# Expert weights through two queues: places 1, 3 and 5 of a round loaded by GpSimd, the other four by SP

## What is computed

```python
N_EXPERTS = 8; TOP_K = 2; EXPERT_FF = 3584

def _swiglu(x, w1, w3, w2):
    return (jax.nn.silu(x @ w1) * (x @ w3)) @ w2

def _moe(x, w_router, w1, w3, w2):
    logits = (xt @ w_router).astype(jnp.float32)
    top_v, top_e = lax.top_k(logits, TOP_K)
    gates = jax.nn.softmax(top_v, axis=-1)
    # every expert e: y[tokens that chose e] += gate * _swiglu(x[those tokens], w1[e], w3[e], w2[e])
```

## Time and profile before

| | us |
|---|---|
| median of the runs | 3134.4 |
| lowest and highest | 3132.83, 3137.07 |
| the profiled execution | 3133.49 |
| its span, first to last instruction | 3131.8 |
| from the first expert's first up product to the end of the last | 850.8 to 1677.0 |
| TensorE busy in the span | 3082.3 |
| DMA queue q1 (SP) | 703.62 MB |
| DMA queue q0 (GpSimd) | 8.02 MB |

### The profile page before, as it was taken

The page is one execution under the profiler, slowest core; times in us unless marked ns, Lnnn a source line. Parts: engine busy times, 40 slices in busy tenths (PEclk is TensorE's granted clock), DMA queues, the critical chain, the costliest instruction groups (busy, mean ns, idle before and its releaser), DMA issues.

```text
span 3131.8 us, 79620 instructions
## 1 busy us (share of the span) xinstructions
PE 3082.3 (98%) x36280; PEld 2622.5 (84%) x36280; DVE 1326.7 (42%) x2660; ACT 445.9 (14%) x1079; POOL 53.9 (2%) x87
## 2 busy tenths in 40 slices
PE   9999999999999999999998999999999999999998
PEld 6686894978599999999997967898995976999894
DVE  2252566543201110111014665754566565654465
ACT  1250000042111111111111001211100001111100
POOL 0000000000000000000000000000000000000000
PEclk9999999999999999999999999999999999999999
DMA  7434443432699999999996444433444444434442
GB/s 261 143 114 161 162 161 145 186 132 106 251 416 423 426 426 427 426 426 426 427 426 243 176 164 177 151 144 136 175 175 152 179 160 162 176 135 162 151 172 87
DMA packets 63239, 716.24 MB, mean 229 GB/s; under 512 B 7584, under 2 KB 9248, under 8 KB 11904
## 3 DMA queue, kind: packets, MB, share of 16 engines
q1 hardware_dynamic: 59328, 703.62, 57.0%
q0 software_dynamic: 1152, 8.02, 0.7%
q10 hardware_dynamic: 2624, 2.65, 0.4%
HBM read 711.38 MB, written 1.05 MB: 227 GB/s over the span
## 4 chain that ended last, share of the span: by engine, by line
PE 93%; DMA 4%; DVE 2%; ACT 1%; issue 1%; POOL 0%; SPq 0%; POOLq 0%; DVEq 0%; ACTq 0%
PE psum L647 50%; PE psum L838 13%; PE psum L768 10%; PE psum L848 7%; PE psum L904 4%; DMA weight_ring<-in_experts 4%; PE psum L1166 1%; PE psum L868 1%; PE psum L1259 1%; PE psum L813 1%; PE psum L685 1%; PE psum L681 1%; PE psum L975 0%; PE psum L680 0%; POOL statistics L566 0%
## 5 line engine op out<-in xcount | busy, mean ns | idle before, releaser
L647 PE MATMUL psum<-arena,weight_ring 128*128 128x128 f32 (+1 forms) x6752 | 938.6, 299 | 9.0 <-DVE arena L2302 5.3
L647 PEld LDWEIGHTS psum<-arena,weight_ring 128*128 128x128 f32 x6752 | 881.2, 192 | 53.4 <-issue 14.9
L838 PE MATMUL psum<-arena,weight_ring 128*64 128x80 f32 x14336 | 531.3, 233 | 8.8 <-ACT arena L1461 6.3
L838 PEld LDWEIGHTS psum<-arena,weight_ring 128*64 128x64 f32 x14336 | 510.0, 137 | 13.4 <-ACT arena L1461 7.6
L647 PE MATMUL psum<-weight_ring,arena 128*128 128x128 f32 (+4 forms) x3264 | 494.7, 309 | 2.7 <-DVE arena L2071 2.7
L647 PEld LDWEIGHTS psum<-weight_ring,arena 128*128 128x128 f32 x3264 | 431.4, 191 | 55.5 <-issue 34.3
L1877 DVE TENSOR_TENSOR arena<-arena,psum 128x80 f32<-128x80 f32 x224 | 53.4, 238 | 691.0 <-ACT arena L1451 691.0
L848 PE MATMUL psum<-arena,weight_ring 128*64 128x80 f32 x7168 | 281.7, 233 | 2.3 <-issue 2.3
L848 PEld LDWEIGHTS psum<-arena,weight_ring 128*64 128x64 f32 x7168 | 263.0, 137 | 2.7 <-issue 2.7
L1451 ACT ACTIVATE arena<-psum 128x80 f32<-128x80 f32 x224 | 53.4, 238 | 642.8 <-PE psum L838 642.8
L904 PE MATMUL psum<-weight_ring,arena 128*128 128x512 f32 x320 | 138.8, 592 | 0.0
(11 more groups left out here) (292 smaller groups left out, 2367.8 us busy)
## 6 DMA issues: line engine op xcount, KB each, us to landing
weight_ring<-in_experts SPq DMA_DIRECT2D x224, 1536.0 KB, 14.5
weight_ring<-in_ffn_up SPq DMA_DIRECT2D x44, 2048.0 KB, 7.7
weight_ring<-in_second_wide SPq DMA_DIRECT2D x42, 2048.0 KB, 7.8
weight_ring<-in_first_wide SPq DMA_DIRECT2D x35, 2048.0 KB, 8.8
weight_ring<-in_ffn_down SPq DMA_DIRECT2D x20, 2048.0 KB, 7.8
weight_ring<-in_dense_up SPq DMA_DIRECT2D x11, 2048.0 KB, 8.0
weight_ring<-in_dense_down SPq DMA_DIRECT2D x5, 2048.0 KB, 8.0
weight_ring<-in_ffn_down SPq DMA_DIRECT2D x4, 1024.0 KB, 5.2
```

The costliest lines, as they stand in the source:

```text
L647: m = pe.matmul(o, lhs, rhs, start=i == 0, stop=i == len(terms) - 1)
L838: mm = pe.matmul(psum[g * STRIP:(g + 1) * STRIP, q % 4, m * CAP:(m + 1) * CAP], w[:, m, k, g * STRIP:(g + 1) * STRIP], chosen[:, k, :], st ...
```

## The change

Places 0, 2, 4 and 6 of a round are still loaded by SP, through the same loops with a step of two. Places 1, 3 and 5 are loaded by GpSimd with the same waits, from loops of the same form, which stand in its program behind the load of `late_gate` and ahead of the first layer norm root after the experts. Buffers, semaphores, bytes and every other engine's program stay.

```diff
-            for q in range(ROUND):
+            for q in range(0, ROUND, 2):
                 sp.wait_ge(unit_used, MOE_START - SLOTS + 1 + q // 2)
                 sp.dma_start(expert_unit(q), a["experts"][q * P:(q + 1) * P, :]).then_inc(expert_loaded[q], 16)
             def load_round(e, g):
-                for q in range(ROUND):
+                for q in range(0, ROUND, 2):
                     sp.wait_ge(expert_used, ROUND * (ROUNDS * e + g) + q - ROUND + 1)
                     sp.dma_start(expert_unit(q), ...).then_inc(expert_loaded[q], 16)
...
+            def load_round(e, g):
+                for q in range(1, ROUND, 2):
+                    pool.wait_ge(expert_used, ROUND * (ROUNDS * e + g) + q - ROUND + 1)
+                    pool.dma_start(expert_unit(q), a["experts"][bass.ds((e * EXPERT_UNITS + ROUND * g + q) * P, P), :]).then_inc(expert_loaded[q], 16)
...
                     pool.dma_start(late_gate, ...)
+                if l == 1:
+                    for q in range(1, ROUND, 2):
+                        pool.wait_ge(unit_used, MOE_START - SLOTS + 1 + q // 2)
+                        pool.dma_start(expert_unit(q), a["experts"][q * P:(q + 1) * P, :]).then_inc(expert_loaded[q], 16)
+                    with pool.Fori(1, ROUNDS) as g:
+                        load_round(0, g)
+                    with pool.Fori(1, EXPERTS) as e:
+                        with pool.Fori(0, ROUNDS) as g:
+                            load_round(e, g)
                 for h in range(HALVES):
                     layernorm_root(l, 1, h)
```

## The result

| | before | after |
|---|---|---|
| median of the runs | 3134.1 us (4 runs, 3132.8 to 3137.1) | 3161.9 us (4 runs, 3160.2 to 3164.3) |
| profiled execution | 3133.5 us, span 3131.8 | 3162.6 us, span 3160.9 |

The ratio is 1.0085, with a 95% interval of 1.0071 to 1.0099: slower by 0.85%, far over the 0.2% that can be told from no change. The forecast was 3138 us with a range up to 3152; the time lies outside it.

The account below looks back on a forecast made before the run. Transfers were taken to bound the expert stage. Issuing, rate and start-up at 0 and order at +3.5 us gave 3133.5 + 3.5 = 3137.0 us, with 0.9 us for the median 3138 us; range 3131 to 3152 us.

Parts of the forecast that it names:

- What bounds the kernel: Expert stage: from the third or fourth expert on, transfers are the bound, by 1.2 us per expert over TensorE.
- Issuing at 0: Expert stage: GpSimd sits idle for 854.9 us, nothing useful queues behind the new waits, so issuing there costs 0.
- Rate at 0: Expert stage: both queues together move 427 GB/s as one does; 0 taken, ends -6.7 and +18 us, 8.0 us per cent.
- the engines get slower: Rival, expert stage: GpSimd's descriptors must be written and fetched, slowing the engines; 1% is 8.0 us, 3146 us; chance 0.10.
- Order at +3.5 us: Stage's end: GpSimd's units land early and SP's late, leaving TensorE more work after the last landing; +3.5 us.
- three SP loads left: Pattern at the stage's end: 219 lands at T - 7.38 us and five units remain, 9.2 us after T; +5.9 us.
- Start-up at 0: Expert's end: GpSimd's later start, some 4 us on busy engines, is just hidden by the cover; 0.
- a cover of 4.9 us: Expert's end: about 4.9 us of data the engines still hold when slots are freed again at 1579.7 us.
- that rival: Engines run dry after each expert, TensorE's delay shrinking the cover; about 10 us over seven ends plus 3.5, 3148 us; chance 0.27.
- the rate rival: Expert stage: the engines get slower with GpSimd's descriptors; 1% is 8.0 us; chance 0.10.
- 422 or less with visible dips after each expert: Sign in the stage's rate, in GB/s, that the engines run dry; lower everywhere would mean slower engines.
- The sign for the order: Rate stands and the last load leaves TensorE two or more units; its waits come at even places, SP's.

Follow-up runs that it names:

- the kernel with one load held back: Kernel before, all expert loads by SP, but the first load after an expert's start waits for two more used units: 3155.5 us, ratio 1.0068.
- even split: Against the kernel before, SP loads even units and ScalarE odd ones, counted over the whole run: 3136.5 us, ratio 1.0008.
- one place: Against the kernel before, GpSimd loads only place 3 of every round, 32 of 224 loads: 3137.8 us, ratio 1.0009.
- the disorder kept away from the ends: Against the kernel before, ScalarE loads places 1, 3 and 5 in rounds 1 and 2 of each expert only, SP the rest: 3135.0 us, ratio 1.0002.
- the swap: The change with places exchanged, GpSimd loading 0, 2, 4, 6 and SP 1, 3, 5: 3153.2 us, ratio 1.0061 against the kernel before.

## Why the prediction was wrong, point by point

**What bounds the kernel: right.** The transfers bound the stage, and each microsecond in which the engines are dry is paid: 2.5 us of gap, 2.7 us of a longer expert, in the kernel with one load held back.

**Issuing at 0: right for the stage, wrong for the program.** The conditions and the root behind them cost nothing. But I counted what a GpSimd load costs where it is issued and not what it leaves behind for the end. The drain, 1.49 us in the kernel before, had a cover of 3.5 us; 7.84 us more exposed 4.5. The step that failed is "Cost 0" under issuing; I had not looked at GpSimd's last instruction.

**Rate at 0: half right.** Two busy queues can run at 426 GB/s (even split, one place). But in this split packets were slow after each gap, 7.6 us in all by the packets' own times, near the 8.0 us that I gave to 1%. It is neither in the rate of two GpSimd loads beside SP's nor in a slower engine everywhere, and the rival "the engines get slower" had another mechanism in mind: the last 76 us of the expert ran at 427. Most of it falls where at most two expert loads were in flight, so it belongs to the engines' running dry more than to the rate. A slip besides: eight times 102.1 and 3 is 819.8 and not 819.5 us, so the most that could be gained was 6.4 us and not 6.7.

**Order at +3.5 us: right mechanism, too small and put in one place only.** At the stage's end the measured +4.5 us (9.2 left instead of 4.7) lies between my +3.3 and the +5.9 us for three SP loads left; the chain with five units after the wait is that pattern. That its 9.2 us came out to the tenth is luck: the five units took 17.9 us and not 16.6, because six sets of down products and not five lay in them, and began 8.8 us before the last landing and not 7.4. For the same reason the 3.3 us that I set against it were too few; my own gave 4.7. The failing step is that this term was booked once, at the end. The same delay of TensorE against the transfers comes at each expert's end, where it takes the cover. I wrote this down as a rival and left it out of the sum. The runs show it as the main thing: with the order kept, or the disorder kept away from the ends, nothing is lost.

The Trainium skill (DMA: Bandwidth & Descriptors, Queues, rings and completion order) says that each engine takes turns, packet by packet, between the queues that have work for it. By that rule the queue with three places of seven gets half the engines while both have loads, and the trace agrees: from 1231 to 1242 us q0 took 50.2% and q1 50.5% of the engines' time, and the loads take 12.3 us to landing against 16.3. The same page's Rules for kernel authors say that spreading transfers over issuing engines doesn't help bandwidth and saves issue time only. That there was nothing to gain the runs bear out; here the spreading cost 0.85%.

**Start-up at 0: the step that failed most.** It rested on a cover of 4.9 us, read in a kernel whose order the change itself alters. With it spent, both queues' starts are exposed. The rival's figures were a cover of 1.4 us for SP's first load and 1.8 us for GpSimd's; measured gaps are 1.35 and 0.91 us in the third expert, so both covers were shorter than thought: SP's own start is exposed too, which I had left out. From its issue to full engines GpSimd's load took 3.4 us (SP's 2.0), near the some 4 us of the earlier trace rows. From the freed slot (the down products end at 1067.40 + 1.28 = 1068.7 us for SP and 1070.72 + 1.28 = 1072.0 for GpSimd) to full engines it took 2.3 us with SP and 4.2 us with GpSimd, 1.9 us more, just about the "some 2 us" from which I said the rival decides. In the swap, where GpSimd's load met idle engines, it was 3.0 us (1280.0 to 1283.0), so the extra is not a fixed one. The condition was right and I put it on the wrong side, with a chance of 0.27.

**The size of that rival.** I gave it 3148 us: 10 us for seven ends and 3.5 for the order. The measured parts are 11.6 us dry and 4.5 us at the end, so these two terms were nearly right, 16.1 against 13.5 us. The rest, 7.6 us of slow packets and 4.5 us of drain, was in no case of mine, and a bit of clock, 1.5 us, is on top. A range that had taken the rate rival and this one together, which nothing forbade, would have reached 3148 + 8 = 3156 us, and still missed the drain.

**What would show it: it did.** I had named "422 or less with visible dips after each expert" as the sign of engines that run dry. The slices read 404 to 425, with the dips where said. The sign for the order held too: 20 units were begun within 0.25 us of their landing, all of them at even places, SP's, and in 14 of the cases a later unit had landed already (none of 23 before). That experts would stay at 103.3 us did not hold.

No version here beats the kernel before. That fits the first reading: one queue keeps the engines at 100.9%, and no split tried here reached the 6.4 us that TensorE could give at most.

## What to carry to other kernels

A buffer ring that is consumed in order wants its loads to land in order. If it must be fed by two queues, give them loads in strict turn, so that both hold the same number; in a group of odd length a fixed choice of places breaks that. This was shown with ScalarE as the second engine, where it cost nothing and gained nothing. A cover read in the trace of before is worth only as much as the change leaves of it: when a change delays the consumer at a boundary, take that delay off the cover first and then ask of each queue whether its start still fits. And a term found at the end of a stage is to be looked for at each inner boundary of the same kind.

## What the runs showed of the hardware

- GpSimd's closing drain grew by 0.082 us for each load that it had issued, from 1.49 us at 10 loads over 4.10 at 42 to 9.33 at 106, whether the added loads were of 1, 8 or 1536 KB. With 138 and 234 loads it was 2.22, 1.57 or 9.82 us. It costs only what reaches beyond the last work of the others: 4.5 of 7.84 us in the kernel after, nothing for the 4.10 us of 42 loads (its end at 3134.4 us, the span's at 3135.3).
- Many tiny transfers beside a stream at the ceiling cost far more than their bytes: 68 loads of 1 KB took 5.0 us from the stream, 0.07 us each.
- The 12-KB packets were slower where few loads were in flight: 464 ns with four, 476 (before, one queue) to 515 ns (after) with two, and 412 GB/s at a DMA share of 1.00 for 12 to 16 us after a dip in either kernel. With three loads issued at once behind a longer gap it was 428 GB/s. No cause was found.
- The stretches of lower granted clock lie at different places from one execution to the next: 0.66 over 831 to 836 us before and 1.00 after, 1.00 over the first group behind the stage before and 0.82 after.
